# Weight blocks in halves, additions before weight splits, and a reordered first stage in a float32 decoder step

## What is computed

```python
mkv = [_mem_kv(mem_prompt, norm_mem_kv[l], mem_w_k[l], mem_w_v[l]) for l in range(DEPTH)]
# trunk, layer 0: pooling mixer; layer 1: dilated attention into shared keys and values
h = _rmsnorm(x, norm_mix[l])
u = h @ pool_w_in[l]
x = x + _pool_mix(u_ext, t, pool_w_group[l], pool_scale[l]) @ pool_w_out[l]      # l == 0
x = x + _dilated_mix(h, dil_w_q[j], dil_w_o[j], attend)                          # l == 1
x = x + _mem_attend(_rmsnorm(x, norm_mem_q[l]), mem_k[l], mem_v[l], mem_w_q[l], mem_w_o[l])
x = x + _swiglu(_rmsnorm(x, norm_ffn[l]), ffn_w_gate[l], ffn_w_up[l], ffn_w_down[l])
```

## Time and profile before

| | us |
|---|---|
| median of 3 runs | 2376.31 (2375.81 to 2376.61) |
| the profiled execution | 2376.49 |
| its span, first to last instruction | 2374.6 |
| PE busy | 2319.3 (98%) |
| DVE busy | 1308.8 (55%) |
| ACT busy | 911.1 (38%) |
| POOL busy | 114.4 (5%) |
| DMA, mean over the span | 182 GB/s |

### The profile page before, as it was taken

The page is one execution under the profiler, slowest core; times in us unless marked ns, Lnnn a source line. Parts: engine busy times, 40 slices in busy tenths (PEclk is TensorE's granted clock), DMA queues, the critical chain, the costliest instruction groups (busy, mean ns, idle before and its releaser), DMA issues.

```text
span 2374.6 us, 44090 instructions
## 1 busy us (share of the span) xinstructions
PE 2319.3 (98%) x19160; PEld 2283.6 (96%) x19160; DVE 1308.8 (55%) x1310; ACT 911.1 (38%) x777; POOL 114.4 (5%) x131
## 2 busy tenths in 40 slices
PE   7999999999999999999999999989999999999998
PEld 6899998999999999999999998889999999999998
DVE  7578555655445554455546764565554455544554
ACT  6433444433333333333444334543333333333333
POOL 0000111100000000000101021120000000000001
PEclk9999999999999999999999999999999999999999
DMA  7565664555555555555556456545555555555553
GB/s 240 195 195 170 222 201 172 165 181 183 179 177 177 177 178 182 185 179 177 178 187 209 152 199 232 178 155 183 177 177 177 180 183 181 180 178 177 177 180 123
DMA packets 376208, 433.22 MB, mean 182 GB/s; under 512 B 7936, under 2 KB 344144, under 8 KB 375582
## 3 DMA queue, kind: packets, MB, share of 16 engines
q1 hardware_dynamic: 365838, 397.50, 51.2%
q0 software_dynamic: 9552, 33.68, 4.0%
q10 hardware_dynamic: 720, 0.58, 0.1%
HBM read 426.21 MB, written 6.45 MB: 182 GB/s over the span
## 4 chain that ended last, share of the span: by engine, by line
PE 88%; issue 4%; DVE 3%; DMA 2%; ACT 2%; POOLq 1%; DVEq 0%; POOL 0%; SPq 0%; ACTq 0%
PE acc L757 28%; PE acc L759 28%; PE acc L758 28%; DVE wlo L1233 1%; POOLq L1835 1%; ACT whi L456 1%; DMA raw<-in_pool_w_out 1%; PE ab L1004 0%; PE acc L835 0%; PE acc L856 0%; DMA raw<-in_dil_w_q 0%; PE acc L836 0%; PE acc L837 0%; DMA raw<-in_mem_w_v 0%; DMA raw<-in_mem_w_k 0%
## 5 line engine op out<-in xcount | busy, mean ns | idle before, releaser
L1233 DVE TENSOR_TENSOR wlo<-raw,whi 128x2048 fp32r<-128x2048 f32 x372 | 851.5, 2291 | 592.4 <-ACT whi L456 571.2
L757 PE MATMUL acc<-xs,whi 128*128 128x264 f32 (+1 forms) x3776 | 1081.6, 286 | 6.8 <-DVE x L1288 3.1
L759 PE MATMUL acc<-xs,wlo 128*128 128x264 f32 (+1 forms) x3776 | 1073.4, 284 | 0.0
L758 PE MATMUL acc<-xs,whi 128*128 128x264 f32 (+1 forms) x3776 | 1072.7, 284 | 0.0
L456 ACT ACTIVATE whi<-raw 128x2048 fp32r<-128x2048 f32 x372 | 710.3, 1912 | 897.6 <-DMA raw<-in_ffn_w_up 327.8
L757 PEld LDWEIGHTS acc<-xs,whi 128*128 128x128 f32 x3776 | 709.9, 188 | 8.3 <-DVE x L1288 3.8
L759 PEld LDWEIGHTS acc<-xs,wlo 128*128 128x128 f32 x3776 | 713.6, 189 | 0.0
L758 PEld LDWEIGHTS acc<-xs,whi 128*128 128x128 f32 x3776 | 711.2, 188 | 0.3
L757 PE MATMUL acc<-hA,whi 128*128 128x264 f32 (+1 forms) x1216 | 347.0, 285 | 6.0 <-ACT tmp L656 2.1
L759 PE MATMUL acc<-hA,wlo 128*128 128x264 f32 (+1 forms) x1216 | 345.7, 284 | 0.0
L758 PE MATMUL acc<-hA,whi 128*128 128x264 f32 (+1 forms) x1216 | 344.9, 284 | 0.0
(11 more groups left out here) (289 smaller groups left out, 1152.1 us busy)
## 6 DMA issues: line engine op xcount, KB each, us to landing
raw<-in_ffn_w_gate SPq DMA_DIRECT2D x88, 1024.0 KB, 5.0
raw<-in_ffn_w_up SPq DMA_DIRECT2D x88, 1024.0 KB, 5.0
raw<-in_ffn_w_down SPq DMA_DIRECT2D x88, 1024.0 KB, 5.3
raw<-in_dil_w_q SPq DMA_DIRECT2D x24, 1024.0 KB, 5.0
raw<-in_pool_w_in SPq DMA_DIRECT2D x16, 1024.0 KB, 5.3
raw<-in_pool_w_out SPq DMA_DIRECT2D x16, 1024.0 KB, 5.4
raw<-in_mem_w_v SPq DMA_DIRECT2D x8, 1024.0 KB, 7.8
raw<-in_mem_w_k SPq DMA_DIRECT2D x8, 1024.0 KB, 5.1
```

The source lines that it names most:

```text
L757: mm(out, w_hi, hi_, start=first, stop=False)
L758: mm(out, w_hi, lo_, start=False, stop=False)
L759: return mm(out, w_lo, hi_, start=False, stop=last)
L1233: v.tensor_tensor(wlo[:, n % NSPLIT, :], raw[:, n % NSPLIT, :], whi[:, n % NSPLIT, :].bitcast(F32), ALU.subtract).then_inc(lo_ready, 1)
```

## The change

1. A weight block is loaded, copied and subtracted in two halves, with a semaphore for each half; PE waits for the half that it needs next. The second load half of a block that was used by rows still waits for its own half; after a block used by columns both wait for the whole.
2. In the first stage PE makes 12 products of ones before the memory rows have landed. The gains are turned between the two halves of the memory rows. value_phase makes all products with the high weights of a block first and those with the low weights after them. x, the pooling state and the memory keys are turned through the banks ab, between halves of memk0's, memv1's and win's blocks. DVE's and ACT's work there is put into another order, and the sums of squares of x are taken in halves.
3. zF gets eight places in xs_flat, and the wait for h_ready goes.
4. In the memory attention DVE's splits of mo+2 and mo+3 stand behind the attention; within mo an addition stands ahead of each split, and there is one split less.
5. The first splits of dq stand apart, with low columns between.

```diff
-    ("memload", 0, 4),
-    ("xload", 0, 1),
-    ("memv0", 4, 1), ("xt", 0, 5), ("st", 0, 2),
-    ("memk0", 4, 2), ("memv1", 4, 1), ("memkt0", 0, 1), ("memk1", 4, 2), ("memkt1", 0, 1),
+    ("memload0", 0, 2), ("xload", 0, 1), ("memload1", 0, 2),
+    ("memv0", 4, 1), ("memk0", 4, 2), ("memv1", 4, 1), ("memk1", 4, 2),
...
-        zF = tmp[:, 0:4 * T].rearrange("p (j m t) -> p j m t", j=2, m=2)
+        zF = xs_flat[:, 0:16 * T].rearrange("p (j m t) -> p j m t", j=8, m=2)
...
-                if n >= NSPLIT:
-                    eng.wait_ge(half_used, 2 * (n - NSPLIT + 1))
                 if n == N0["do"] + 2:
                     eng.wait_ge(v_used, VU0["dil"] + 4)
                 src = weight_source(n)
-                eng.dma_start(raw_as(n % NSPLIT, src.shape[1]), src).then_inc(raw_in[n % NSPLIT], 16)
+                nk = src.shape[1]
+                for half in range(2):
+                    if n >= NSPLIT:
+                        eng.wait_ge(half_used, 2 * (n - NSPLIT) + (2 if by_columns(n - NSPLIT) else 1 + half))
+                    ks = slice(half * nk // 2, (half + 1) * nk // 2)
+                    eng.dma_start(raw_as(n % NSPLIT, nk)[:, ks, :], src[:, ks, :]).then_inc(raw_in[n % NSPLIT][half], 16)

             def loop_blocks(name, turns, per, source):

-                with eng.Fori(0, turns) as i:
+                peeled = 1 if by_columns(N0[name] - 1) else 0
+                for j in range(per * peeled):
+                    load_block(N0[name] + j)
+                with eng.Fori(peeled, turns) as i:
                     for j in range(per):
                         n = N0[name] + j
-                        eng.wait_ge(half_used, 2 * per * i + 2 * (n - NSPLIT + 1))
                         src = source(i, j)
-                        eng.dma_start(raw_as(n % NSPLIT, src.shape[1]), src).then_inc(raw_in[n % NSPLIT], 16)
+                        for half in range(2):
+                            eng.wait_ge(half_used, 2 * per * i + 2 * (n - NSPLIT) + 1 + half)
+                            ks = slice(4 * half, 4 * half + 4)
+                            eng.dma_start(raw_as(n % NSPLIT, 8)[:, ks, :], src[:, ks, :]).then_inc(raw_in[n % NSPLIT][half], 16)
...
-                landed(eng, n, more)
-                nc.scalar.activation(whi[:, n % NSPLIT, :], raw[:, n % NSPLIT, :], ACT.Copy).then_inc(hi_ready, 1)
+                for half in range(2):
+                    landed(eng, n, half, more)
+                    nc.scalar.activation(half_block(whi, n, half), half_block(raw, n, half), ACT.Copy).then_inc(hi_ready, 1)
...
+                upto(N0[f"mo{l}"] + 3)
                 for i in range(4):
-                    upto(N0[f"mo{l}"] + min(i + 3, 5))
                     for j in range(2):
                         high_tiles(gen, 4 * i + 2 * j, G0[f"mo{l}"] + 2 * i + j)
+                    if i:
+                        upto(N0[f"mo{l}"] + min(i + 3, 5))
...
                 samples_exp(0)
-                upto(mo + 3)
                 samples_exp(1)
...
-            upto(N0["memk0"])
...
+            upto(N0["memk0"] + 1)
...
-            upto(N0["memk0"] + 3)
+                for half in range(2):
+                    x_rows_sum(c, half)
+                upto(N0["memk0"] + 2 + c)
...
-                    eng.wait_ge(h_ready, 8 + (2 * gi - 1 + j if gi else 0))
...
+                        last = nc.scalar.activation(zF[:, 2 * gi + j, m, :], acc[:, 2 * (g % 2) + m, 0:T], ACT.Copy, scale=gains[:, c:c + 1])
...
+            upto(N0["dq"])
             side_copy(SIDE["kt"] + 1, stage2[0:TS, 0:MEMD])
-            upto(N0["dq"] + 1)
...
-            def block_ready(n, more=0):
-                eng.wait_ge(hi_ready, more + (n + 1))
-                eng.wait_ge(lo_ready, more + (n + 1))
+            def block_ready(n, half, more=0):
+                eng.wait_ge(hi_ready, more * 2 + (2 * n + half + 1))
+                eng.wait_ge(lo_ready, more * 2 + (2 * n + half + 1))
...
-                    block_ready(n + i, nmore)
                     for k in range(8):
+                        if k % 4 == 0:
+                            block_ready(n + i, k // 4, nmore)
...
-                    block_ready(n + i)
+                    block_ready(n + i, 1)
...
-                    block_ready(n + i)
                     s = (n + i) % NSPLIT
                     for k in range(4):
+                        if k % 2 == 0:
+                            eng.wait_ge(hi_ready, 2 * (n + i) + k // 2 + 1)
                         if ready is not None:
                             ready(4 * i + k)
...
+                        w_hi = whi[:, s, k * 512:(k + 1) * 512]
+                        for c in range(2):
+                            x_hi, x_lo = (part[:, c * P:(c + 1) * P] for part in (tile or xtile)(4 * i + k))
+                            mm(acc[:, 2 * (g % 2) + c, :], x_hi, w_hi, start=i == k == 0, stop=False)
+                            mm(acc[:, 2 * (g % 2) + c, :], x_lo, w_hi, start=False, stop=False)
+                    for k in range(4):
+                        if k % 2 == 0:
+                            eng.wait_ge(lo_ready, 2 * (n + i) + k // 2 + 1)
+                        w_lo = wlo[:, s, k * 512:(k + 1) * 512]
+                        for c in range(2):
+                            x_hi = (tile or xtile)(4 * i + k)[0][:, c * P:(c + 1) * P]
+                            last = mm(acc[:, 2 * (g % 2) + c, :], x_hi, w_lo, start=False, stop=i == 3 and k == 3)
                         if k % 2 == 1:
...
+            eng.wait_ge(ones_ready, 1)
+            for i in range(12):
+                mm(acc[:, 3, 0:P], ones[:, :], ones[:, :], start=True, stop=True)
...
-            eng.wait_ge(gains_in, GAINS_IN)
-            turn_item(G0["xload"], [(P, 0, P, gain_rows[:, 0:P]), (P, 1, 48, gain_rows[0:48, P:2 * P])])
-
-            def memory_keys_out(l):
+                    turn_item(G0[f"memload{c}"] + j, [(P, m, P, cached(("mem", c))[:, (8 * j + m) * P:(8 * j + m + 1) * P])
+                                                      for m in range(8)])
+                if c == 0:
+                    eng.wait_ge(gains_in, GAINS_IN)
+                    turn_item(G0["xload"], [(P, 0, P, gain_rows[:, 0:P]), (P, 1, 48, gain_rows[0:48, P:2 * P])])
...
+                side_turn(SIDE["mk"] + l, [(P, 4 * c + h, P, mKT[:, l, h, c * P:(c + 1) * P])
+                                           for c in range(2) for h in range(NH_MEM)])
...
+            def turn_x(i):
+                c, j = divmod(i, 2)
...
+                side_turn(SIDE["xt"] + i, [(P, m, P, cached(("x", c))[:, (8 * j + m) * P:(8 * j + m + 1) * P]) for m in range(8)])
...
+            def turn_state(j):
...
+                side_turn(SIDE["st"] + j, [(P, m, TS * NST, cached(("state", 0), j)[0:TS * NST, m * P:(m + 1) * P])
+                                           for m in range(8)])
+
+            value_phase("memv0", None, xs_wait("memkv0"), lambda: row_statistics(STAT["mem"], 1, False))
+            pair_item(N0["memk0"], G0["memk0"], 2, xtile, width=TP,
+                      halves={0: lambda: turn_x_samples(), 1: lambda: turn_x(0), 2: lambda: turn_x(1), 3: lambda: turn_x(2)})
+            pair_item(N0["memk0"] + 2, G0["memk0"] + 1, 2, xtile, width=TP,
+                      halves={0: lambda: turn_x(3), 1: lambda: turn_state(0), 2: lambda: turn_state(1)})
+            value_phase("memv1", htile, lambda k: eng.wait_ge(low_ready, k + 1), lambda: turn_memory_keys(0))
             pair_phase("memk1", 2, 2, htile, width=TP)
-            memory_keys_out(1)
-            pair_phase("win", 8, 2, xtile, xs_wait("mix0"), after_first=lambda: row_statistics(STAT["mix0"], 2, True))
+            pair_item(N0["win"], G0["win"], 2, xtile, xs_wait("mix0"),
...
             def lo(n, more=0):

-                eng.wait_ge(hi_ready, more + (n + 1))
-                v.tensor_tensor(wlo[:, n % NSPLIT, :], raw[:, n % NSPLIT, :], whi[:, n % NSPLIT, :].bitcast(F32),
-                                ALU.subtract).then_inc(lo_ready, 1)
+                for half in range(2):
+                    eng.wait_ge(hi_ready, more * 2 + (2 * n + half + 1))
+                    v.tensor_tensor(half_block(wlo, n, half), half_block(raw, n, half), half_block(whi, n, half).bitcast(F32),
+                                    ALU.subtract).then_inc(lo_ready, 1)
...
             v.memset(eps[:, :], EPS)
...
+                if c == 0:
+                    eng.wait_ge(turned, TURN0["xload"] + 1)
+                    v.tensor_copy(gains[:, :], acc[:, 2 * (G0["xload"] % 2), 0:176]).then_inc(acc_free, 1)
             eng.drain()
...
-            lo(0)
-            at[0] = 1
...
-                if m in (3, 7, 11):
-                    upto(1 + m // 4)
+                if m % 4 == 3:
+                    upto(m // 4)
             rms(STAT["mem"], TP, 2)
+            for m in range(6):
+                low_memory(m)
             upto(N0["memk0"])
-            for m in range(10):
...
+            x_samples_turned()
```

(26 more changed lines are left out.)

148 lines of the change are left out of this document (66 added, 82 removed).

## The result

The changed kernel takes 2342.77 us (median of four runs, 2341.24 to 2346.19) for 2376.06 (2374.11 to 2376.61): a ratio of 0.9863, interval 0.9846 to 0.9880. The forecast was 2345.0, in 2339 to 2359. The two profiled executions are 2376.49 and 2343.64 us, 32.85 apart.

The account below looks back on a forecast made before the run. PE bounds the kernel, busy 2319.3 of 2374.6 us; losses lie in a few short places. Terms 9.5, 2.2, 2.0, 10.6, 2.1 and 5.5 make 31.9, less 0.4: 31.5 off 2376.49 gives 2345.0, range 2339 to 2359.

Parts of the forecast that it names:

- Halving costs nothing on PE: All 372 blocks: added PE semaphore waits taken as 0; ACT 75 and DVE 35 us more work, costed at nothing in loops.
- Rivals 3 and 4: Added half boundaries cost PE time (at 0.1 us, 2382; chance 0.03); halved transfers served in turn (3890 or 2397; chance 0.02).
- First stage: Start to about 125 us: earlier first product, shorter low clock, turns between half blocks, fewer waits; -9.5 us, bounds 6.5 and 12.
- the sixteen high products cover this nearly: At memv1's first block, 3.7 us of high products nearly hide DVE's split, some 4 us late; 0.9 us of wait left.
- Group products: Turn from pooling to group products: the wait of ACT's scaled copy for DVE's pooling goes entirely, -2.2 us.
- Late blocks: At 259 to 290 and 1262 to 1292: half transfers asked for 2.9 us earlier, splits done 2 us sooner; -2.0 us.
- Memory attention: Both memory attentions and their output products: moved splits, clock kept up, earlier additions and squares; 5.4 and 5.2, together -10.6 us.
- Query start: At 1234 to 1262: dq's first columns wait for one halved split, not two whole ones; -2.1 us.
- Output product: Dilated attention's output product, 1449.8 to 1516: halves cut a chain turn from 7.06 to 6.25 us; -5.5 us, lowest 3.
- (1): Gains overlap less: low clock in memv0, memv1 delay and late blocks stay, output product gives 3; 2353 us, chance 0.22.
- (2): Gains overlap more: clock does not fall in memv0, all 7 us come at the output product; 2341 us, chance 0.12.
- (5): New waits for side_free, low columns and moved splits eat the gain; 2374 us, chance 0.03.

Follow-up runs that it names:

- the four pieces: Changed kernel with every weight block in four transfers, copies and subtractions, and PE waiting at each quarter: 2343.39 us.
- after: The changed kernel itself, all parts of the change made to the original kernel: 2342.77 us, ratio 0.9863.
- both whole: Changed kernel in its new order, but with one transfer, one ACT copy and one DVE subtraction per block: 2356.44 us.
- before: The original kernel without the change: 2376.06 us.
- the last kernel: Changed kernel plus memv1's first split ahead of low columns, with 46 and 42 products of ones of 32 columns, the 42 ahead of memv0: 2369.93 us.
- the kernel with three places put back: Changed kernel with zF in tmp, mo+2 and mo+3 splits among the attention heads, and both dq splits first, as originally: 2359.42 us.

## Why the prediction was right, point by point

**Halving costs nothing on PE**: shown by the four pieces. ACT's half takes 1.06 us (1.1 forecast), DVE's 1.23 (1.15 to 1.2). ACT's busy time rose by 52.6 us for 75. The fit that the forecast weighed, from the Trainium skill (DMA: Bandwidth & Descriptors, Anatomy of one DMA), 2.0 us fixed plus the bytes at 436 GB/s, gives an estimate of 3.2 us for a half and 2.6 for a quarter; the profiles show 3.5 and 2.9. So the fit is near for one transfer, and what was drawn from it, that two in a row would take their sum, falls: 512 KB transfers at 3.5 us pass twice per 5.85 us. Rivals 3 and 4 are out. (In rival 4, 3.0 us a half would cost 372 x 0.15 = 56 us and not 52.)

**First stage, 9.1 for 9.5.** Start 15.31 for 14.8 and memk0 at 39.74 for 38.4: both too early, by 0.5 and 1.3. The memory rows stood turned at 14.0, inside the 13.5 to 14.3 of the text; the step that failed is the one behind it, a high and a low column, 1.3 us to PE's start and not 0.5 to 1. The stretch at the lower level was about halved, 3.4 us of memv0 for 6.0, as forecast, but not by the products of ones: these speed up the turns. The turns between halves brought 5.4 us up to the end of memk0 (28.66 for 34.1 from 42.25 to 76.35), for 4.2: a turn that stands between products puts PE off by 0.8 us (46.20 to 46.99 in after) and not by 1.0. The two errors cancel. And the step "the sixteen high products cover this nearly" carried more than it said: without it the stage would have been worth next to nothing. The forecast's sum has a slip too: its last term stands as 1.7 us in one sentence and as 1.5 in the sum.

**Group products, 2.3 for 2.2**: right, all of the wait went. Undone in the new kernel it costs 4.2, since the clock then falls as well.

**Late blocks, 2.6 for 2.0**: right in size, wrong in one of its two reasons. The transfer that is asked for earlier brings nothing by itself (the kernel with whole transfers has no such wait). At the first late block the splits in halves do: whole splits cost 2.1 us there. At the second either half is enough: whole splits alone cost nothing, both whole 0.8.

**Memory attention, 12.3 for 10.6.** 6.3 and 6.0: 3.8 from the place of the two splits with the clock that no longer falls, 2.5 from additions ahead of splits and from the halves. The steps of the forecast had 2.2 + 1.4 for the one and 1.1 + 0.7 for the other, so the mis-sized term is the second; by the earlier trace rows its stretch idled 1.93 us, and all of that and 0.6 more went. The forecast gave it to the additions alone; the kernel before with halves alone shows that halves bring 1.5 of it too.

**Query start, 1.5 for 2.1**: 0.29 and 0.20 us of waits are left where the forecast took all.

**Output product, 5.6 for 5.5**, by terms that were off. The turn is 6.55 us and not 6.25: two DVE halves are 2.65 us, where the sum had them beside ACT's copy at the cost of a whole, 2.29. Eight turns at 0.51 are 4.1 us of the chain; the rest fits the clock, which is at 1.00 where it was 0.97.

**Not in the forecast**: the dilated samples, put at no change, lost 0.7 us: a stand-still of 1.64 us, less what the clock gave back (no lower level there in after, 3.4 us in before). So part of the nearness of 2342.8 to 2345.0 is luck: terms of 1 to 2 us each that were off, or that chance decides, partly cancel.

The rest of the rivals: (1) and (2) were in the range and not needed; DVE did delay memv1, by 0.88. (5), no gain, is out by the table. Of the forecast's signs the first product of win stands at 115.67 us for about 115.

## What to carry to other kernels

A split in two stages, one engine copying and the next subtracting, is worth halving where a chain of waits runs through it, even when the transfers stay whole; where PE was fully busy it cost nothing here, with ACT at no more than 266 and DVE at 323 of 600 us; what it costs where they are full, no run shows. Let PE first do what needs only the earlier of two operands: here that order hid some 9 us that the other moves had put ahead of it. And count with the clock at every long wait: behind waits of 2.4 to 2.9 us it fell in some kernels and not in others, for 3.4 us and so at a price of about 1.7 us each time. Fillers in idle time may keep it up: with ten products of ones ahead of memv0 it stayed in two kernels of two, and in the last kernel it fell among them.

## What the runs showed of the hardware

The same idle time ahead of memv0, 2.81 us, was followed by a fall of the granted clock in after and in the kernel with three places put back, and by none in the kernels with four pieces and with whole splits. Such a term, about 1.7 us, can be there or not from one kernel to the next, and from one execution to the next: the mean clock of after's four is 0.997 to 1.000.

PE's transposes alone raised the clock: it rose at 8.98 in before, which had made nothing else. The records followed each other after 0.21 us up to there and after 0.11 behind it.

A product of ones into the same bank, made again and again before the clock rose, takes about 0.2 us a record with 32 columns as with 128. The weight load beside it is one of 128 x 128 in both.

PE can stand still 0.2 to 2.9 us at a place that belongs to its code and not to its data, until 1.3 to 1.5 us behind the landing of a 16,384-byte transfer of the instruction queue; a change elsewhere moves the place. In the kernel with whole transfers that and the clock behind it are 3.8 of the 4.4 us by which its trace is longer, so differences of 2 or 3 us between kernels like these say nothing of the edit unless the trace shows them at the edit.
